# In the stage of the first tiles, ACT makes the first tap of a tile's conv ahead of the silu of the tile before it, from the fifth tile on

## The chip, the cores and the metric

The kernel runs on one core of a Trainium2 chip. The metric is the device time of one execution in microseconds. Five engines work from queues of their own and meet at semaphores: TensorE (PE), VectorE (DVE), ScalarE (ACT), GpSimd (POOL) and SyncE (SP), which issues nearly all DMAs. Each engine takes its instructions in the order in which the kernel lists them.

## The reference

Two transformer blocks run one after the other on 512 tokens of width 1024 (the first adds 16 meta tokens, which makes 528). The change touches only the head of the first block:

```python
h = rmsnorm(h_res, norm1_w)
proj = h @ w_in                       # q, k, v (1024 columns each), z, b, a, ...
qkv = silu(depthwise_conv_centred(concat([q, k, v]), conv_w))   # 5 taps along the tokens
q, k = l2norm(q) * 128 ** -0.5, l2norm(k)       # 8 heads of 128
o = chunk_gated_delta_rule(q, k, v, g, beta)    # forward and backward
```

The delta rule needs, for each chunk and head, products of k with k and with q, the inverse of a triangular matrix made of them, and k and v with the tokens on the partitions.

## The kernel before

Channels lie on the partitions and tokens along the free axis. Matrices are cut in units of 128 output columns by 1024 inputs. To come near float32 with the fast number format, each unit is split in a rounded part `w_hi` (ACT, `round_unit`, line 383) and the rest `w_lo` (POOL, `split_unit`, line 389), and so are the activations; a product is three passes, hi by hi, lo by hi, hi by lo (`gemm`, line 401).

The stage of the first tiles runs over the 24 entries of `TILES`: 0 to 3 are heads 0 to 3 of k, 4 to 7 heads 0 to 3 of q, 8 to 11 and 12 to 15 heads 4 to 7 of k and q, and 16 to 23 the eight heads of v. Every engine has a loop over n = 0 to 24 in its own program, and all loops list their work tile by tile. For tile n:

- PE (`pe_program`, from line 1437) makes 48 matmuls into one of two pairs of PSUM banks, pair n % 2. It first waits until the conv of tile n-2 has read that pair (`cv`, four increments per tile). The last matmul raises `s_pe` to n+1.
- ACT (`act_program`, line 1741, loop from line 1768) rounds the weights of unit n+2, makes the silu of tile n-1 (line 1774, it waits for the four steps of conv n-1 and raises `si`), and then the first of the five taps of tile n (line 1783): a scaled copy from PSUM to the buffer `cacc[:, n % 2]`. The tap waits for `s_pe` at n+1 (for tiles 0 to 3, for DVE's scaling of the tile, `fd`), and for silu n-2, which was the last to read that buffer. It raises `m_tap`. Then come the square of q for a q tile (line 1794) and ACT's part of the side tasks.
- DVE (`dve_program`, line 2100) waits for `m_tap` and adds the other four taps (line 2148), each a pass over the tile, then its side tasks.
- POOL splits unit n+2, SP loads the weights of unit n+4.

The table `SIDE` puts other work behind tile n on every engine: transposes of k at n = 4, 5, 10 and 12 (`pe_kt`, line 639, each for two heads), products and exponentials of the chunks (`pg`, `pk`, lines 498 to 567), the inverse of the blocks on DVE in eight parts at n = 16 to 23 (`sub_part`, lines 604 to 618), and transposes of v at n = 18, 20, 22 and 24 (`pe_vt`, line 700, two heads each). `pe_kt` and `pe_vt` wait for the silus of their heads. At n = 10, 12, 18, 20 and 22 the two heads are tiles n-2 and n-1; at n = 4, 5 and 24 the heads are tiles 0 and 1, 2 and 3, 22 and 23. `pe_pk` at n = 8 waits for silu 7. In PE's queue all this lies between gemm n and gemm n+1. ACT's functions use several tables; a table load (`ACT_TABLE_LOAD`) stands directly ahead of the first instruction that needs another table.

When DVE has copied the inverse (`raw<-inv`, line 618), SP writes it to memory and loads it for the next stage, the chunks of the delta rule, which PE opens with line 875 at 240 us.

Of the kernel before, what the change touches and what calls it, by code (L numbers as in the profile page):

```python
# [10 lines left out]
ACT = mybir.ActivationFunctionType  # L11
# [7 lines left out]
HALF = T1 // 2  # L19
# [61 lines left out]
TILES = [("k", h) for h in range(4)] + [("q", h) for h in range(4)] + [("k", h) for h in range(4, 8)] + [("q", h) for h in range(4, 8)] + [("v", h) for h in range(8)]  # L81
# [44 lines left out]
def build(nc, a, out):  # L126
    ctx = ExitStack()
    with ctx:
        def sem(name):
            return ctx.enter_context(nc.semaphore(name))  # L130
# [25 lines left out]
        def z(name, shape, off, dt=F32):  # L156
            n = int(np.prod(shape[1:])) * 4
            assert z0 + off + n <= nc.sbuf_usable_end, (name, z0 + off + n, nc.sbuf_usable_end)
            return at(name, shape, z0 + off, dt)
# [55 lines left out]
        cacc = z("cacc", [P, 2, T1], W2)  # L215
# [63 lines left out]
        ps = ctx.enter_context(nc.psum_tensor("ps", [P, 8, 512], F32))  # L279
# [4 lines left out]
        def pcol(name, tile, tap=0):  # L284
            o, n, k = PAR[name]
            return par[:, o:o + n * k].rearrange("p (n k) -> p n k", k=k)[:, tile, tap:tap + 1]
# [4 lines left out]
        def pair(v):  # L291
            return v.rearrange("p (b n) -> p b n", b=2)
# [11 lines left out]
        QKV = {"q": ("cq", qT), "k": ("ck", kT), "v": ("cv", vT)}  # L304
# [3 lines left out]
        s_hi, s_lo, s_pe = sem("s_hi"), sem("s_lo"), sem("s_pe")  # L308
# [8 lines left out]
        si = Signal(sem("s_si"), t=3 * H)  # L317
# [10 lines left out]
        fd = Signal(sem("s_fold"), n1=5, gu=2 * FT, lr=2 * LT)  # L328
# [26 lines left out]
        m_tap, m_eg, m_de, m_kme, m_ksq, m_nk = (Mark(sem(f"m_{n}")) for n in ("tap", "eg", "de", "kme", "ksq", "nk"))  # L355
# [21 lines left out]
        def round_unit(e, u):  # L377

            if u < NU:
                e.wait_ge(s_raw[u % RAW], 16 * (u // RAW + 1))  # L380
                if u >= RAW:
                    e.wait_ge(s_pe, u - RAW + 1)
                e.activation(w_hi[:, u % RAW, :], w_raw[:, u % RAW, :], ACT.Copy).then_inc(s_hi, 1)  # L383
# [64 lines left out]
        def query(n):  # L448

            return None if not 0 <= n < len(TILES) or TILES[n][0] != "q" else TILES[n][1]  # L450

        def decays():
            return ps[:, 7, 0:3 * NB * 2 * H].rearrange("p (i c n) -> p i c n", i=3, c=NB)
# [200 lines left out]
        def act_kt(e, hf):  # L654
            e.wait_ge(*m_ktm.at(hf))
            e.wait_ge(*hh.at("n1", KT))
            e.activation(k_met[0:META, HG * hf:HG * hf + HG, :], bankv(4, META, P), ACT.Copy).then_inc(m_kme.sem, 1)

        def act_n2(e, hf):
            e.wait_ge(*m_kte.at(HG * hf + 3))  # L660
            e.wait_ge(*m_kme.at(hf))
            if hf:
                e.wait_ge(*m_nc.at(1))
            e.activation(ksq[:], k_tok[:, hf].rearrange("p c u m -> p (c u) m"), ACT.Square).then_inc(m_ksq.sem, 1)
            e.activation(ksq_m[0:META], k_met[0:META, HG * hf:HG * hf + HG, :], ACT.Square).then_inc(m_ksq.sem, 1)
# [1075 lines left out]
        def act_program(e):  # L1741
            o, n, _ = PAR["norm1"]
# [20 lines left out]
            def first_hi(k):  # L1763
                e.wait_ge(*hh.at("n1", k + 1))
                e.activation(h_hi[:, k, :], hf0[:, k, :], ACT.Copy).then_inc(hi.sem, 1)


            for n in range(len(TILES) + 2):
                if n < len(TILES):
                    round_unit(e, n + 2)  # L1770
                if 1 <= n <= len(TILES):
                    what, h = TILES[n - 1]
                    e.wait_ge(*cv.at("t", 4 * n))
                    e.activation(QKV[what][1][:, h, :], cacc[:, (n - 1) % 2, :], ACT.Silu).then_inc(si.sem, 1)
                if n < len(TILES):
                    what, h = TILES[n]
                    b = 2 * (n % 2)
                    for k in (0, 1, 2) if n == 2 else ():
                        first_hi(k)
                    e.wait_ge(*(fd.at("n1", (1, 2, 4, 5)[n]) if n < 4 else (s_pe, n + 1)))  # L1780
                    if n >= 2:
                        e.wait_ge(*si.at("t", n - 1))
                    e.activation(pair(cacc[:, n % 2, :]), ps[:, b:b + 2, 0:HALF], ACT.Copy, scale=pcol(QKV[what][0], h)).then_inc(m_tap.sem, 1)  # L1783
                    if n == 2:
                        for k in range(3, KT):
                            first_hi(k)
                i = query(n - 1)
                if i is not None:
                    e.wait_ge(*si.at("t", n))
                    if i >= HG:  # L1790
                        e.wait_ge(*m_qs.at(0))
                    if i == HG:
                        e.wait_ge(s_qn, 16)
                    e.activation(qsq[:, i % HG, :], qT[:, i, META:T1], ACT.Square).then_inc(sq.sem, 1)
                for task, arg in SIDE.get(n, ()):
                    if task == "bat":
                        e.wait_ge(*dg.at("b", 1))
                        e.activation(beta[:], beta[:], ACT.Sigmoid).then_inc(ga.sem, 1)
                        e.activation(small[:, 32:48], small[:, 0:16], ACT.Exp).then_inc(ga.sem, 1)
                        e.wait_ge(*dg.at("ch", 3))  # L1800
                        e.activation(tmpc[:, 1, :], tmpc[:, 1, :], ACT.Exp).then_inc(ga.sem, 1)
                    if task == "dk":
                        e.wait_ge(*pg.at("dk", 1))
                        for i in range(3):
                            e.activation(tabs[:, i], decays()[:, i], ACT.Exp if i else ACT.Copy).then_inc(ga.sem, 1)
                    if task == "ktm":
                        act_kt(e, arg)
                    if task == "ks":
                        act_n2(e, arg)
                    if task == "nk":  # L1810
                        act_nk(e)
                    if task == "vt":
                        act_vt(e, arg)
                    if task == "vtm":
                        act_vtm(e, arg)
                    if task == "msa":
                        act_msa(e, arg)
                    if task == "msb":
                        act_msb(e, arg)
                    if task == "pg":  # L1820
                        act_pg(e, arg)
                    if task == "qs":
                        act_qs(e, arg)
                    if task == "mk":
                        act_mg(e)
# [222 lines left out]
            for g in range(LT // 3 + 1):  # L2048
                n, last = 7 * g + BASE["xr0"], g == LT // 3
# [666 lines left out]
```

## Time and profile before

| | us |
|---|---|
| median of 3 runs | 1828.39 |
| lowest and highest | 1827.64, 1830.20 |
| the profiled execution, its own time | 1829.92 |
| its span | 1828.1 |
| PE busy | 1747.4 |
| DVE busy | 824.5 |
| ACT busy | 679.7 |
| POOL busy | 861.4 |
| mean granted clock of PE | 0.975 |

The span is what the profiler recorded, from the first instruction to the last; the time of an execution holds a little more. Every row of a timeline gives the start in us from the start of the span, the length in us, engine, line, operation and the tiles written and read (`out<-in`); x8 says that eight instructions were merged. In brackets stands how long the engine had stood idle and who released it.

### The profile page before, as it was taken

The page shows a single profiled execution, that of the slowest core. Times are in us where ns is not written, and L with a number is a line of the kernel's source. Part 1 is how long each engine was busy: PE and PEld are TensorE (multiplying, and loading weights), DVE is VectorE, ACT ScalarE, POOL GpSimd, SP SyncE. Part 2 cuts the span into 40 slices and gives each one's busy share as a digit, 9 for nine tenths or more (in the row PEclk, how much of TensorE's full clock was granted, in tenths as well). Part 3 has the DMA queues.
Part 4 walks back from the last instruction along what each step waited for, and adds up shares of the span by engine and source line. Part 5 has one row for each costly group of instructions (what it writes and reads, how often), then busy time and mean ns, then how long its engine had stood idle before and what let it go on. Part 6 is the DMA issues. An engine that isn't in the chain of part 4 may idle for free.

```text
span 1828.1 us, 22823 instructions
## 1 busy us (share of the span) xinstructions
PE 1747.4 (96%) x9151; PEld 1473.5 (81%) x9151; DVE 824.5 (45%) x1323; ACT 679.7 (37%) x997; POOL 861.4 (47%) x482
## 2 busy tenths in 40 slices
PE   7899869999999999999999999989999999999987
PEld 7888869998988888877888878868887788877766
DVE  7668925923323301122111121127999842457642
ACT  5656523332332222233222232233233443365651
POOL 3356423232334644544555554445477645456552
PEclk9899969999999999999999999989999989999998
DMA  5475258463422324222222223322222312222222
GB/s 193 136 226 164 70 155 254 133 173 110 145 70 71 96 98 140 92 93 92 93 93 92 93 92 104 104 70 93 94 98 89 112 58 93 92 93 92 93 74 76
DMA packets 120145, 201.41 MB, mean 110 GB/s; under 512 B 32448, under 2 KB 71512, under 8 KB 120040
## 3 DMA queue, kind: packets, MB, share of 16 engines
q1 hardware_dynamic: 118552, 197.47, 34.3%
q10 hardware_dynamic: 1488, 2.48, 0.4%
q8 instruction: 73, 1.20, 0.3%
q14 instruction: 32, 0.26, 0.0%
HBM read 170.46 MB, written 29.46 MB: 109 GB/s over the span
## 4 chain that ended last, share of the span: by engine, by line
PE 85%; DVE 9%; ACT 3%; issue 2%; DMA 1%; POOL 1%; SPq 0%; DVEq 0%; ACTq 0%
PE ps L401 67%; PE ps L1733 3%; DVE cacc L2148 2%; PE ps L875 2%; PE ps L921 1%; PE ps L928 1%; PE ps L907 1%; PE ps L885 1%; PE ps L915 1%; PE ps L883 1%; PE ps L932 1%; PE ps L893 1%; DVE inv L615 1%; DVE ps L1341 1%; PE ps L1680 1%
## 5 line engine op out<-in xcount | busy, mean ns | idle before, releaser
L389 POOL TENSOR_TENSOR w_lo<-w_raw,w_hi 128x1024 fp32r<-128x1024 f32 x264 | 632.8, 2406 | 567.0 <-ACT w_hi L383 566.9
L401 PE MATMUL ps<-hp_hi,w_hi 128*128 128x512 f32 (+2 forms) x1664 | 558.2, 363 | 7.3 <-DVE cacc L2148 6.1
L401 PE MATMUL ps<-hp_lo,w_hi 128*128 128x512 f32 (+2 forms) x1664 | 553.3, 360 | 0.0
L401 PE MATMUL ps<-hp_hi,w_lo 128*128 128x512 f32 (+2 forms) x1664 | 553.2, 360 | 0.0
L401 PEld LDWEIGHTS ps<-hp_hi,w_hi 128*128 128x128 f32 x1664 | 297.7, 191 | 63.2 <-issue 7.5
L401 PEld LDWEIGHTS ps<-hp_lo,w_hi 128*128 128x128 f32 x1664 | 297.1, 190 | 50.3 <-issue 1.7
L401 PEld LDWEIGHTS ps<-hp_hi,w_lo 128*128 128x128 f32 x1664 | 297.4, 190 | 48.0
L383 ACT ACTIVATE w_hi<-w_raw 128x1024 fp32r<-128x1024 f32 x264 | 277.5, 1053 | 152.0 <-DMA w_raw<-in_w 144.3
L1221 DVE SCALAR_TENSOR_TENSOR ps<-u_in,par,ps 128x511 f32<-128x511 f32 (+14 forms) x240 | 176.7, 739 | 8.4 <-ACT ps L1213 0.8
L2148 DVE SCALAR_TENSOR_TENSOR cacc<-ps,par,cacc 128x528 f32<-128x528 f32 x96 | 73.6, 767 | 37.3 <-ACT cacc L1783 34.6
L2524 POOL TENSOR_TENSOR y_lo<-tmp,y_hi 128x512 fp32r<-128x512 f32 x22 | 28.4, 1289 | 105.6 <-ACT y_hi L1932 105.6
L401 PE MATMUL ps<-y_hi,w_hi 128*128 128x512 f32 x176 | 69.6, 396 | 1.5 <-DVE tmp L2284 1.5
L1929 ACT ACTIVATE tmp<-tmp 128x512 f32<-128x512 f32 x22 | 13.9, 632 | 150.8 <-DVE tmp L2277 150.8
L401 PE MATMUL ps<-y_hi,w_lo 128*128 128x512 f32 x176 | 69.5, 395 | 0.0
L401 PE MATMUL ps<-y_lo,w_hi 128*128 128x512 f32 x176 | 69.5, 395 | 0.0
L2279 DVE TENSOR_TENSOR ps<-ps,tmp 128x512 f32<-128x512 f32 x22 | 15.4, 699 | 103.8 <-PE ps L401 103.8
L401 PE MATMUL ps<-mx_hi,w_hi 128*128 128x512 f32 x144 | 57.4, 398 | 0.0
L401 PE MATMUL ps<-mx_lo,w_hi 128*128 128x512 f32 x144 | 57.1, 397 | 0.0
L401 PE MATMUL ps<-mx_hi,w_lo 128*128 128x512 f32 x144 | 57.0, 396 | 0.0
L2277 DVE TENSOR_TENSOR tmp<-tmp,ps 128x512 f32<-128x512 f32 x22 | 15.1, 687 | 92.5 <-PE ps L401 85.7
L943 ACT ACTIVATE TR<-ps 128x512 f32<-128x512 f32 x32 | 19.1, 597 | 89.9 <-PE ps L875 89.9
L2309 DVE TENSOR_TENSOR x<-x,ps 128x512 f32<-128x512 f32 x8 | 5.5, 686 | 102.1 <-PE ps L401 102.1
(397 smaller groups left out, 2575.5 us busy)
## 6 DMA issues: line engine op xcount, KB each, us to landing
w_raw<-in_w SPq DMA_DIRECT2D x264, 512.0 KB, 3.5
d_y<-zero SPq DMA_DIRECT2D x6, 688.0 KB, 6.1
d_x<-zero SPq DMA_DIRECT2D x6, 688.0 KB, 5.9
d_at<-at SPq DMA_DIRECT2D x16, 256.0 KB, 3.0
d_kc<-kc SPq DMA_DIRECT2D x16, 256.0 KB, 3.2
d_qd<-eg SPq DMA_DIRECT2D x16, 256.0 KB, 3.1
d_p<-dec SPq DMA_DIRECT2D x16, 256.0 KB, 3.4
AT<-d_at SPq DMA_DIRECT2D x16, 256.0 KB, 6.1
```

Of the source, the lines that this page charges most:

```text
L383: e.activation(w_hi[:, u % RAW, :], w_raw[:, u % RAW, :], ACT.Copy).then_inc(s_hi, 1)
L389: e.tensor_tensor(w_lo[:, u % RAW, :], w_raw[:, u % RAW, :], w_hi[:, u % RAW, :].bitcast(F32), ALU.subtract).then_inc(s_lo, 1)
L401: mm = e.matmul(ov, w, r[:, k, t0:t1], start=(first and n == 0 and p3 == 0), stop=(last and n == len(tiles) - 1 and p3 == 2))
L615: e.tensor_tensor(inv[:, j + 1:, 0:w], inv[:, j + 1:, 0:w], prd, ALU.subtract).then_inc(m_sub.sem, 1)
L875: mm = e.matmul(bankv(LB[s], P, P)[:, u], SQ[s]["AT"][:, u], SQ[s]["X"][:, u], start=True, stop=True)
L883: e.matmul(half_cols(LB[s], 0)[:, u], T[:, u], blocks(Y, 1 - s)[:, u], start=True, stop=True)
L885: mm = e.matmul(half_cols(LB[s], 1)[:, u], Y[:, u], blocks(T, s)[:, u], start=True, stop=True)
L943: e.activation(SQ[s]["TR"][:], bankv(LB[s], P, P), ACT.Copy).then_inc(q_tc[s].sem, 1)
L1221: e.scalar_tensor_tensor(acc[:, t:SEQ], u_in[:, k, 0:SEQ - t], pcol("ca", k, TAPS - 1 - t), acc[:, t:SEQ], ALU.mult, ALU.add).then_inc(cl. ...
L1733: mm = e.matmul(ps[:, LBANK[j], :], w, r[:, k, :], start=(k == 0 and p3 == 0), stop=(k == LT - 1 and p3 == 2))
L2148: e.scalar_tensor_tensor(acc, ps[:, b:b + 2, t:t + HALF], pcol(QKV[what][0], h, t), acc, ALU.mult, ALU.add).then_inc(cv.sem, 1)
L2524: e.tensor_tensor(y_lo[:, j - 1, :], row(2 + (j - 1) % 2), y_hi[:, j - 1, :].bitcast(F32), ALU.subtract).then_inc(lo.sem, 1)
```

## The change

From the fifth tile on (n = 4), ACT makes tap n before silu n-1; before, the silu came first. The tap's code moves into a function `act_tap`, with the same waits and the same operands. For n below 4 the order stays. The other engines' programs are untouched. Nothing is added or taken away.

```diff
+            def act_tap(n):
+
+                what, h = TILES[n]
+                b = 2 * (n % 2)
+                e.wait_ge(*(fd.at("n1", (1, 2, 4, 5)[n]) if n < 4 else (s_pe, n + 1)))
+                if n >= 2:
+                    e.wait_ge(*si.at("t", n - 1))
+                e.activation(pair(cacc[:, n % 2, :]), ps[:, b:b + 2, 0:HALF], ACT.Copy, scale=pcol(QKV[what][0], h)).then_inc(m_tap.sem, 1)
 
             for n in range(len(TILES) + 2):
                 if n < len(TILES):
                     round_unit(e, n + 2)
+                if 4 <= n < len(TILES):
+                    act_tap(n)
                 if 1 <= n <= len(TILES):
                     what, h = TILES[n - 1]
                     e.wait_ge(*cv.at("t", 4 * n))
                     e.activation(QKV[what][1][:, h, :], cacc[:, (n - 1) % 2, :], ACT.Silu).then_inc(si.sem, 1)
-                if n < len(TILES):
-                    what, h = TILES[n]
-                    b = 2 * (n % 2)
+                if n < 4:
                     for k in (0, 1, 2) if n == 2 else ():
                         first_hi(k)
-                    e.wait_ge(*(fd.at("n1", (1, 2, 4, 5)[n]) if n < 4 else (s_pe, n + 1)))
-                    if n >= 2:
-                        e.wait_ge(*si.at("t", n - 1))
-                    e.activation(pair(cacc[:, n % 2, :]), ps[:, b:b + 2, 0:HALF], ACT.Copy, scale=pcol(QKV[what][0], h)).then_inc(m_tap.sem, 1)
+                    act_tap(n)
```

## Rows read from the trace of the kernel before

**Rows 1.** The page, part 1: busy time, share of the span, instructions.

```profile
PE 1747.4 (96%) x9151; PEld 1473.5 (81%) x9151; DVE 824.5 (45%) x1323; ACT 679.7 (37%) x997; POOL 861.4 (47%) x482
```

**Rows 2.** Busy time in two stretches: PE, PEld, DVE, ACT, POOL, granted clock, DMA.

```profile
168.00:228.00 60.00, 55.67 (x410) 50.60 (x409) 56.19 (x101) 31.90 (x73) 29.41 (x42) 0.97 0.23 72
300.00:1828.00 1528.00, 1489.09 (x7243) 1227.54 (x7241) 617.39 (x918) 527.73 (x742) 729.46 (x372) 0.99 0.31 99
```

**Rows 3.** The chain of waits at the end of the stage: start, length, what.

```profile
213.42 7.70 PE ps L401 x48
221.14 0.71 ACT cacc L1783
...
226.49 1.05 DVE raw L618
...
240.10 2.05 PE ps L875 x8
```

**Rows 4.** The tap's line 1783: its waits, and who waited for it.

```profile
  PE ps L401: 27.7, 12
...
  DVE cacc L2148: 34.6, 13
```

**Rows 5.** Timeline of ACT at tile 14.

```profile
150.32 1.28 ACT L1774 ACT_TABLE_LOAD   x1
...
152.16 0.68 ACT L1783 ACTIVATE cacc<-ps,par 128x528 f32<-128x528 f32 x1
```

**Rows 6.** Timeline of PE behind gemm 8.

```profile
94.20 2.00 PE L507 MATMUL ps<-kT 128*128 128x128 f32 x8 [2.35 <-ACT qT L1774]
```

**Rows 7.** Timeline of ACT at tiles 18, 20 and 22.

```profile
179.88 1.28 ACT L1774 ACT_TABLE_LOAD   x1
181.17 0.64 ACT L1774 ACTIVATE vT<-cacc 128x528 f32<-128x528 f32 x1
182.97 0.70 ACT L1783 ACTIVATE cacc<-ps,par 128x528 f32<-128x528 f32 x1 [1.15 <-PE ps L401]
...
195.51 0.65 ACT L1774 ACTIVATE vT<-cacc 128x528 f32<-128x528 f32 x1 [3.55 <-DVE cacc L2148]
196.06 0.68 ACT L1783 ACTIVATE cacc<-ps,par 128x528 f32<-128x528 f32 x1
...
211.09 0.64 ACT L1774 ACTIVATE vT<-cacc 128x528 f32<-128x528 f32 x1 [5.98 <-DVE cacc L2148]
```

**Rows 8.** Timeline of PE: what lies between the gemms of tiles 18 to 23.

```profile
182.76 1.04 PE L700 MATMUL ps<-cf,vT 128*128 128x128 f32 x8
...
189.62 0.38 PE L706 MATMUL ps<-cf,vT 128*16 128x128 f32 x2
...
195.84 1.04 PE L700 MATMUL ps<-cf,vT 128*128 128x128 f32 x8
...
208.93 0.60 PE L700 MATMUL ps<-cf,vT 128*128 128x128 f32 x4
211.79 0.66 PE L700 MATMUL ps<-cf,vT 128*128 128x128 f32 x4 [2.26 <-ACT vT L1774]
212.38 1.04 PE L818 MATMUL ps<-v_met,m_dec 16*16 16x128 f32 x8
```

**Rows 9.** Timeline of DVE: the convs of tiles 19, 21 and 23.

```profile
192.31 3.17 DVE L2148 SCALAR_TENSOR_TENSOR cacc<-ps,par,cacc 128x528 f32<-128x528 f32 x4
...
207.90 3.17 DVE L2148 SCALAR_TENSOR_TENSOR cacc<-ps,par,cacc 128x528 f32<-128x528 f32 x4
...
221.88 3.18 DVE L2148 SCALAR_TENSOR_TENSOR cacc<-ps,par,cacc 128x528 f32<-128x528 f32 x4 [0.58 <-ACT cacc L1783]
```

**Rows 10.** Busy time in two stretches, columns as in rows 2.

```profile
213.80:217.20 3.40, 3.40 (x17) 3.40 (x16) 3.26 (x6) 2.46 (x8) 0.87 (x1) 0.50 0.00 0
...
94.30:97.70 3.40, 3.40 (x17) 3.40 (x17) 3.26 (x7) 1.90 (x3) 3.32 (x4) 0.50 0.80 304
```

**Rows 11.** Groups of DVE's instructions from 148 to 228 us, costliest first.

```profile
L2148 DVE SCALAR_TENSOR_TENSOR cacc<-ps,par,cacc 128x528 f32<-128x528 f32 x40 | 30.6, 766 | 6.9 <-ACT cacc L1783 5.9
```

## The prediction

> **What bounds the kernel now.** I read the page first: PE is busy 96% of 1828.1 us [rows 1], and from 300 us to the end it stands still for only 39 of 1528 us [rows 2]. What happens before 240 us therefore moves all that follows, one for one. The stage of the first tiles ends at 240.10 us, when PE starts the next stage after standing still since 227 us. The reader sees in the chain of waits what that start hangs on: gemm 23, tap 23, conv 23, the rest of the block solve, the copy `raw<-inv` at 226.49 us, its DMAs, then PE [rows 3]. From 168 to 228 us DVE is busy 56.2 of 60 us and PE 55.7 [rows 2]; the two are nearly level, and either can set the end.
>
> "Gemm n", "tap n", "silu n" and "conv n" mean tile n's 48 matmuls, its first tap on ACT (line 1783), its silu on ACT (line 1774) and its four steps on DVE (line 2148). Over the stage DVE waited 34.6 us for taps, and the taps 27.7 us for PE [rows 4]. So a tap is often late because its gemm is late, and only a tap that stands behind a silu can gain.
>
> **The change part by part.** It adds and removes no instruction. From tile 4 on, 20 taps move ahead of 20 silus, and with each silu its table load, if it has one. The units' rounding stays in front of both, so the weights' loads and POOL's splits keep their place; no DMA moves. Two costs trade places:
>
> - Tap n no longer waits for conv n-1, the load and silu n-1. Gain on DVE.
> - Silu n-1 now waits for gemm n, as tap n does, and whoever wants silu n-1 waits too. Behind it on ACT stand the square of q, the exponentials and the copies. On PE, right behind gemm n, the transposes of k at tiles 10 and 12 and of v at tiles 18, 20 and 22 wait for it: the second of each pair needs silu n-1. The products k·k and q·k behind gemm 8 need silu 7.
>
> *Up to tile 17.* Gain: load and silu 13 stand ahead of tap 14 (150.32 us and 152.16 us [rows 5]), worth 1.8 us. Loss: the transposes behind gemm 10 and 12 wait for their silu, and PE's wait for silu 7, now 2.35 us until 94.20 us [rows 6], grows by a tap of 0.6 us and by about 0.5 us that ACT is already late. By the same steps as below gemm 13 comes some 2.1 us late, half of which hides in waits of PE for DVE's copies, and the exponentials that wait for DVE behind it put ACT 1.8 us back in front of tap 14. Gain and loss cancel: tap 14 stays at 152.2 us. At tile 16 tap 16 (one load and silu earlier) no longer holds DVE, which is then 0.55 us early; this is what the change earns and carries into tile 18. Bounds for this half: -1.8 us (all of the gain) and +2.1 us (none absorbed). I take the cancelled value, since DVE's own work between tiles 14 and 16 is long.
>
> *Tile 18.* Before, load and silu 17 (179.88 and 181.17 us) lie beside gemm 18, and tap 18 waits for PE until 182.97 us [rows 7]. PE runs all eight transposes from 182.76 us and gemm 19 right behind [rows 8]. Now tap 18 stays at 182.97 us, and load and silu 17 follow: 182.97 + 0.60 + 1.28 + 0.65 = 185.5 us (0.60 us is a tap's place in the queue, its 0.70 us less the overlap with the next). Transposes of v1, before at 183.2 us, start at 185.55 us: **PE +2.35 us**. Gemm 19 ends with the row at 189.62 us [rows 8]; it comes to 191.97 us, tap 19 to 192.2 us, conv 19 to 192.9 us. Before it began at 192.31 us [rows 9]; DVE was 0.55 us early, and the loss there is only 0.6 us.
>
> *Tile 20.* Gemm 20 ends at 195.84 us [rows 8] + 2.35 = 198.2 us; tap 20 at 198.4 us, before at 196.06 us right behind silu 19 at 195.51 us [rows 7]. Silu 19 is done at 198.4 + 0.6 + 0.65 = 199.65 us, and the transposes of v3, before at 196.28 us, start there: **PE +3.4 us**. DVE does not feel it: conv 21 follows DVE's own work at 207.90 us [rows 9] + 0.6, while tap 21 is ready at 206.4 us.
>
> *Tile 22.* Gemm 22 ends at 208.93 us [rows 8] + 3.4 = 212.3 us; tap 22 at 212.5, silu 21 done at 212.5 + 0.6 + 0.65 = 213.75 us. Before it ended at 211.09 + 0.65 = 211.74 us [rows 7], and PE waited 2.26 us for it until 211.79 us [rows 8]. That wait swallows 1.4 of the 3.4 us: **PE +2.0 us**. Gemm 23 and tap 23 (221.14 us [rows 3]) and conv 23 (221.88 us [rows 9]) follow at once: 223.9 us. DVE is free at 221.9 us and waits. Nothing behind it has slack: copy, DMAs and PE at 240.10 us come 2.0 us later.
>
> **The sum with the clock as it was: +2.0 us.** The profiled execution took 1829.92 us (span 1828.1 us and 1.8 us around it), 1.5 us above the median of 1828.39 us; such differences between runs are of the size of this result.
>
> *The clock.* Not all of it is fixed. Before gemm 23 PE waited 2.26 us and then made only transposes and matmuls of 16 rows [rows 8]; after that 17 matmuls took 3.4 us at a granted clock of 0.50, the 1.2 GHz level [rows 10]. So gemm 23 took 7.70 us [rows 3] where gemm 19 takes about 6.0 (from the end of the transposes at 183.6 to 189.6 us [rows 8]): one such stretch is worth 1.7 us. PE's wait of 2.35 us from 91.8 us also had one behind it, at 94.3 us [rows 6, 10]. After the change a new wait of 2.35 us with transposes around it stands ahead of gemm 19, as long as the two that had a stretch behind them: I expect one there. On PE's path it adds 1.7 us: gemm 19 ends at 193.7 us, v3's transposes start at 201.4 us, gemm 22 ends at 214.0 us, silu 21 at 215.5 us, everything 1.7 us behind the walk above; DVE, 2.3 us late from conv 19 on, stays just inside. The old stretch may go, since PE's wait ahead of gemm 23 shrinks to 1.1 us; but the light work behind the wait stays. The four cases at the end: none of the two +0.3 us, one of them +2.0 us (either one), both +3.7 us. I take the new one whole and 1.2 of the old one's 1.7 us, **+3.2 us**, nearer to both than to one because only the wait shrinks and not the light work. The Trainium skill's page "TensorE: Matmul & The Clock Gate", Part 1, says the clock falls to half after PE was little busy, and that the monitor runs free of the kernel's start; by it the same wait can have a slow stretch behind it in one run and none in another. The rows agree for two waits; one trace cannot show the second part.
>
> The page "ScalarE: Activation LUTs", section "What ACT_TABLE_LOAD costs", speaks against the change: it puts a switch at 1283 ns and a drain of some 1380 ns more. By it silu 17, moved with its load behind tap 18, would be done 1.38 us later, and the same walk gives +3.4 us where the clock stays as it was. The trace disagrees: silu 17 starts 1.29 us after its load does [rows 7].
>
> **Rivals.**
>
> 1. *More slow stretches.* PE's wait for silu 7 grows to 3.5 us and that for silu 17 is new; each may leave two stretches behind it instead of one. It decides from both stretches of the forecast whole plus any part of a third: 3.7 us, 1832.1 us, at its lower end, 2.0 + 1.7 + 1.7 = 5.4 us, 1833.8 us, with a third, 7.1 us with a fourth. For it: from 168 us on PE has 4.3 us of 60 in which to hide anything [rows 2]. Against: a stretch at 94 us is mostly absorbed by tile 14, as above.
> 2. *The early taps win.* If PE's waits at tiles 18 and 20 stay hidden behind DVE, only the gain stands: 0.55 us at tile 16 and the 0.58 us that DVE waited for tap 23 [rows 9], 1.1 us, 1827.3 us. Against: it needs gemm 23 1.1 us early, and it hangs on silu 21 behind gemm 22. The most that taps can give after 148 us is 6.9 us of DVE's idle time [rows 11], 1821.5 us; that needs PE to be early at every tile.
> 3. *It does nothing.* 12 taps already waited for PE [rows 4], and if the transposes' waits found slack as well, the time stays at 1828.4 us.
> 4. *A load costs more where it follows a tap.* If silu 17 came 1.4 us later than its rows say: 3.4 us on the walk, with the clock's 1.2 us 4.6 us, 1833.0 us.
>
> **How the numbers follow.** A measurement of this kernel can tell about 0.2%, 3.7 us, from no change. Forecast, between +0.3 and +3.7 us: 0.47. Rival 1, from both stretches whole upwards: 0.40. Rivals 2 and 3 within 0.2%: 0.07; rival 2 beyond it: 0.04. Rival 4: 0.02. Predicted: 1828.39 + 3.2 = 1831.6 us. The range starts with the forecast's smallest case, +0.3 us, 1828.7 us, and goes nearly to a fourth stretch, 1835.0 us. Faster 0.04, same 0.47 + 0.07 = 0.54, slower 0.40 + 0.02 = 0.42.
>
> **What the profile would show.** Right: taps 18, 20 and 22 wait for PE with load and silu behind them; PE waits some 2.4 us ahead of the transposes at 183 us and about 1 us at 199 and 213 us; DVE's longest wait late in the stage is the one for tap 23, some 2 us; clock rows of 0.50 stand behind 186 us and perhaps 214 us; `raw<-inv` starts 2 to 4 us later than 226.49 us; behind 240 us everything is shifted and nothing else differs. Wrong: if the transposes at 183 us don't wait, the walk falls at its first step; if they do and the copy is on time, DVE set the end; if the copy is early, rival 2 holds; if it is over 4 us late, the clock's rows say how many stretches.

## The result and the profile after

The changed kernel takes 1832.21 us in the median of 20 runs (1830.37 to 1835.35), the kernel before, run beside it, 1828.07 us (1826.24 to 1831.74, 20 runs). The ratio is 1.0019, with a 95% interval from 1.0013 to 1.0025: 3.5 us more by the ratio (2.4 to 4.6 us), 4.1 us by the medians. Forecast were 1831.6 us and 1828.7 to 1835.0 us.

The profiled execution of the changed kernel took 1830.97 us, its span is 1829.1 us. That is 1.0 us above the span of before, less than the medians differ by. Two things make it so. Of the two slow stretches of PE (stretches at a granted clock of 0.50) that the forecast counted on, this execution had neither. And it was ahead before the new order had cost anything: its conv 6 starts 46.5 us after conv 0, that of before 49.6 us, and a run below with the order of before (e7_before_fill) has 46.6 us as well; before had a slow stretch at 70.4 us that this execution had not. From conv 6 to the copy `raw<-inv` the changed kernel takes 151.2 us and before 148.1 us, 3.2 us more, which is near what the medians say.

The page's first part answers [rows 1]; the windows answer [rows 2, 10] and the second and third rows add the places where the slow stretches had been expected (columns: window, its length, busy time and instructions of PE, PEld, DVE, ACT and POOL, granted clock, DMA share, GB/s):

```profile
PE 1745.7 (95%) x9151; PEld 1470.2 (80%) x9151; DVE 826.8 (45%) x1323; ACT 679.5 (37%) x997; POOL 861.5 (47%) x482
```

```profile
92.00:98.80 6.80, 5.79 (x26) 5.80 (x27) 6.52 (x13) 2.52 (x4) 6.44 (x6) 0.50 0.39 143
184.90:188.30 3.40, 2.95 (x24) 2.96 (x25) 3.23 (x7) 3.40 (x10) 0.10 (x1) 1.00 0.19 70
212.90:217.00 4.10, 3.29 (x26) 2.81 (x27) 3.87 (x8) 4.10 (x15) 0.00 (x0) 1.00 0.39 128
168.00:228.00 60.00, 54.93 (x406) 49.88 (x404) 56.98 (x98) 29.64 (x65) 28.85 (x41) 0.98 0.23 72
300.00:1828.00 1528.00, 1490.10 (x7252) 1227.67 (x7251) 617.88 (x919) 527.75 (x742) 730.32 (x373) 0.99 0.31 99
```

Between 168 and 228 us DVE is busy 0.8 us more than before, PE 0.8 us less. At 185 us and at 213 us the granted clock is 1.00; the stretch at 213.8 us of before [rows 10] is gone. At 92 us PE is at 0.50 for 6.8 us, where before had 3.4 us from 94.3 us on.

On ACT the timeline of the changed kernel at tile 18 answers [rows 7] (start, length, engine, line, operation, tiles; in brackets the idle time before it and who ended it). Line 1774 is now the tap, line 1785 the silu:

```profile
182.64 0.70 ACT L1774 ACTIVATE cacc<-ps,par 128x528 f32<-128x528 f32 x1 [3.10 <-PE ps L401]
183.36 1.28 ACT L1785 ACT_TABLE_LOAD   x1
184.65 0.64 ACT L1785 ACTIVATE vT<-cacc 128x528 f32<-128x528 f32 x1
```

On PE, for silu 7 and for the transposes behind gemm 18, 20 and 22, the same view answers [rows 6, 8]:

```profile
93.00 2.08 PE L507 MATMUL ps<-kT 128*128 128x128 f32 x8 [3.68 <-ACT qT L1785]
182.44 0.60 PE L700 MATMUL ps<-cf,vT 128*128 128x128 f32 x4
185.35 0.66 PE L700 MATMUL ps<-cf,vT 128*128 128x128 f32 x4 [2.31 <-ACT vT L1785]
199.54 0.66 PE L700 MATMUL ps<-cf,vT 128*128 128x128 f32 x4 [0.89 <-ACT vT L1785]
213.71 0.66 PE L700 MATMUL ps<-cf,vT 128*128 128x128 f32 x4 [0.89 <-ACT vT L1785]
```

Each second head's transposes now wait for a silu that stands behind a tap: 2.31, 0.89 and 0.89 us, where the forecast had 2.4, about 1 and about 1. But PE does not set the end in this execution. The chain of waits (start, length, what) runs through DVE, whose shares among the lines between 180 and 245 us are 27.8% for the convs and 42.6% for the block solve; [rows 3] had PE's gemm 23 in its place. Of its pieces:

```profile
188.69 2.48 DVE inv L615
196.00 1.46 DVE prd L612
204.04 1.22 DVE prd L612
217.77 2.49 DVE prd L612
227.15 1.06 DVE raw L618
```

Most steps of the solve at these widths take 0.4 us; these four took 1.2 to 2.5 us. Conv 23 starts at 222.55 us without a wait, the copy `raw<-inv` at 227.15 us, 0.66 us behind [rows 3]. The prediction had named this sign: if the transposes wait and the copy is on time, DVE set the end. From the copy on the two traces are nearly alike (1602.0 us to the end, before 1601.6 us); from 300 us PE is busy for 1490.10 us, 1.0 us more than [rows 2].

### The profile page after: what moved, and what is told of

The parts are those of the page before. It is cut to its first block, busy times and chain, and to the rows that moved or that the text cites. A ratio compares the mean times of both kernels' runs of the same rounds, so it can differ in the third digit from the quotient of the medians.

```text
span 1829.1 us, 22823 instructions
## 1 busy us (share of the span) xinstructions
PE 1745.7 (95%) x9151; PEld 1470.2 (80%) x9151; DVE 826.8 (45%) x1323; ACT 679.5 (37%) x997; POOL 861.5 (47%) x482
## 3 DMA queue, kind: packets, MB, share of 16 engines
q10 hardware_dynamic: 1488, 2.48, 0.4%
## 4 chain that ended last, share of the span: by engine, by line
PE 80%; DVE 8%; issue 2%; ACT 1%; POOL 1%; SPq 0%; DMA 0%; DVEq 0%; ACTq 0%
PE ps L401 64%; PE ps L1733 3%; DVE cacc L2154 2%; PE ps L875 2%; PE ps L921 1%; DVE inv L615 1%; PE ps L928 1%; PE ps L915 1%; PE ps L907 1%; PE ps L885 1%; PE ps L883 1%; DVE prd L612 1%; PE ps L932 1%; PE ps L893 1%; DVE ps L1341 1%
```

## The experiments

A kernel's time is given with its range and number of runs, and the ratio to the kernel before, run on the same chip, with its 95% interval. In the traces I also measured two distances, since a run's start differs by some tenths of a us: the first half is from the start of conv 0 to that of conv 18 (the orders up to tile 17 and their after-effects), the second half from conv 18 to `raw<-inv`. Where another line number stands below, it is the same instruction moved by the inserted lines.

### Which half costs

In the kernel before the silu stands ahead of the tap; here a set, `AHEAD`, says for which tiles the tap stands ahead: 18 to 23 in e1_late, 4 to 17 in e2_early, 14 and 16 in e3_two. The cut shows the edit of the changed kernel.

```diff
-                if 4 <= n < len(TILES):
+                if n in AHEAD:
                     act_tap(n)
...
-                if n < 4:
+                if n < len(TILES) and n not in AHEAD:
```

> The tap stands ahead of the silu only for tiles 18 to 23. My theory (PE's transposes of v wait for the silu that now stands behind the tap, and the clock falls behind the new wait): nearly the whole loss, +2.0 us by the walk at the clock as it was, +2.5 to +4 us with slow stretches; `raw<-inv` at about 228.5 us where gemm 23 has its slow stretch. Rival (the loss is made in the first half, at the wait for silu 7 and at the transposes of k, and its slow stretches): within 0.7 us of the kernel before.

e1_late measured 1833.0 us (1830.9 to 1833.8, 11 runs), ratio 1.0020 (1.0010 to 1.0029), some 3.7 us more, within what was expected of slow stretches. Its profiled execution is the case "both stretches" of the forecast. The chain of waits, then two windows:

```profile
184.56 7.49 PE ps L402 x48
192.28 6.01 PE ps L402 x48
...
215.42 7.69 PE ps L402 x48
223.14 0.71 ACT cacc L1775
...
228.49 1.06 DVE raw L619
```

```profile
185.40:188.80 3.40, 3.40 (x18) 3.40 (x17) 3.30 (x5) 1.46 (x4) 1.86 (x1) 0.50 0.01 2
216.10:219.50 3.40, 3.40 (x18) 3.40 (x17) 3.29 (x5) 1.58 (x4) 1.74 (x1) 0.50 0.00 0
```

Gemm 19 and gemm 23 take 7.49 and 7.69 us beside 6.01 us for gemm 20; tap 23 comes last and DVE waits 1.34 us for it. The second half takes 45.58 us as against 41.83 us before: +3.7 us, the forecast's sum for "both". So the walk on PE through tiles 18, 20 and 22 is borne out, in one execution, for the case in which both stretches fall and PE sets the end.

The same run shows something that had not been looked for. Up to tile 17 its code is that of before, and yet its conv 18 starts 152.9 us after conv 0, where before has 155.8 us. The windows of the two kernels at 70 us, before first:

```profile
70.40:73.80 3.40, 3.40 (x18) 3.40 (x17) 1.39 (x3) 3.37 (x5) 0.85 (x1) 0.50 0.49 181
```

```profile
70.00:77.00 7.00, 7.00 (x59) 6.92 (x58) 1.87 (x4) 5.59 (x9) 2.41 (x1) 1.00 0.32 105
```

One execution had a slow stretch there, the other had none: 18 matmuls in 3.4 us against 59 in 7.0 us. Of the 2.9 us, 1.5 us arise between conv 5 and conv 6, which are 11.0 us apart in before and 9.5 us in e1_late, where this stretch lies. The other 1.4 us are there at conv 5 already; the two executions have slow stretches ahead of it as well, which fall at 22.6 and 56.8 us in before and at 21.5 and 55.7 us in e1_late, but no run isolates their part. The Trainium skill, "TensorE: Matmul & The Clock Gate", Part 1, says that the monitor runs free of the kernel and that the number of slow matmuls varies from run to run; these two rows agree.

> The tap stands ahead of the silu only for tiles 4 to 17. My theory: the half is neutral, gain at tile 16 against losses that are absorbed at tile 14: -0.5 us, up to +1 us if the longer wait for silu 7 leaves a second slow stretch. Rival (the loss is made in this half): +2 to +4 us.

e2_early measured 1832.38 us (1828.77 to 1835.16, 11 runs), ratio 1.0018 (1.0010 to 1.0027). This is a miss, and what the rival had: the first half of the change costs by itself nearly what the whole does. Its trace has PE's wait for silu 7 and, behind it, a slow stretch of 6.8 us (PE's timeline, then the window):

```profile
97.02 2.08 PE L508 MATMUL ps<-kT 128*128 128x128 f32 x8 [3.68 <-ACT qT L1786]
```

```profile
95.80:102.60 6.80, 5.58 (x25) 5.59 (x26) 6.59 (x12) 2.73 (x4) 6.44 (x6) 0.50 0.44 156
```

Conv 18 comes 158.5 us after conv 0, 2.7 us later than before. The two halves cost about 1.0018 and 1.0020 by themselves and 1.0019 together. So they don't add up: a late start of the second half, or its slow stretches, may hide behind one another. That is a reading: the intervals are about 1.7 us to each side, and leave room for this to be scatter.

> The tap stands ahead of the silu at tiles 14 and 16 alone, the two at which no transposes and no products on PE want the silu at once and at which a table load stood ahead of the tap. My theory: the gain without the loss. Tap 14 at about 150.6 us where it was at 152.2, `raw<-inv` about 2.0 us earlier, -1 to -2 us in all. Rival (taps are not what DVE waits for in the long run, since gemm and DVE's own work are level): 0 us within 0.5.

e3_two (only taps 14 and 16, the ones that stood behind a load or a silu without waiting for PE) measured 1828.99 us (1826.91 to 1833.07, 11 runs), ratio 1.0001 (0.9992 to 1.0011): a miss too, no gain shows in the median. In the trace conv 18 is 1.4 us earlier than before (154.4 us after conv 0), and the second half is 1.8 us longer: 0.9 us of it are DVE's waits behind a slow stretch of 6.8 us in place of 3.4 us (window, then DVE's timeline), the other 0.9 us are longer steps of the block solve (see "Where the solve loses it"):

```profile
211.80:218.40 6.60, 6.46 (x28) 5.29 (x29) 6.29 (x12) 5.44 (x16) 1.36 (x1) 0.50 0.04 14
```

```profile
223.45 3.18 DVE L2155 SCALAR_TENSOR_TENSOR cacc<-ps,par,cacc 128x528 f32<-128x528 f32 x4 [1.44 <-ACT cacc L1775]
```

### Does the wait for silu 7 make the first half's loss

```diff
+AHEAD = set(range(4, 24)) - {8}          # e5_not8
+AHEAD = set(range(4, 18)) - {8, 10, 12}  # e6_early_free
```

> The changed order on tiles 4 to 23 except tile 8, where the silu stays ahead of the tap, so that the products behind gemm 8 get silu 7 as before. The half with tiles 4 to 17 lost 3.7 us where I had expected none; its profile and that of the changed kernel show PE waiting 3.7 us for silu 7 and 6.8 us of half clock behind, where the kernel before has 2.35 and 3.4 us. My theory now: this wait and its second slow stretch are what the first half loses, and the second half loses its own 2 to 3.7 us: the whole falls from +4.1 to +2.5 us (within 1.5 to 3.5). Rival (the transposes of k at tiles 10 and 12 make the first half's loss): +4 us as before.

> The changed order on tiles 4 to 17 except tiles 8, 10 and 12, where PE wants the silu right behind the gemm. My theory: the loss of the first half sits in these three; without them it is gone: -1.3 to +0.5 us. Rival (something else of the first half costs, such as the later squares of q or exponentials): +2 us or more.

e5_not8 measured 1833.32 us (1832.89 to 1834.66, 7 runs), ratio 1.0027 (1.0016 to 1.0039): a miss. e6_early_free measured 1831.83 us (1825.55 to 1833.36, 11 runs), ratio 1.0009 (0.9998 to 1.0021), which decides nothing. The premise of both failed, as PE's timeline of e5_not8 shows:

```profile
95.01 2.08 PE L508 MATMUL ps<-kT 128*128 128x128 f32 x8 [3.09 <-ACT qT L1786]
```

With tap 8 behind silu 7 again, PE still waits 3.09 us (3.09 us in e6_early_free as well), not 2.35 us [rows 6]: 0.6 us of the 1.3 us more came from the tap of tile 8, the rest from the earlier tiles, after which ACT is late. Both have a slow stretch of 6.8 us at 94 us. Removing one tap takes only half of the growth away.

### PE kept busy in its waits

To take the clock out of the comparison, PE gets matmuls to do where it stands and waits; their results are overwritten. Their number is chosen to fit into the wait. In both functions the wait for the silu now stands behind them, and the waits for free PSUM banks ahead of them.

```diff
@@ helper
+        def keep_busy(e, bank, count, width=HALF + 4):
+            for _ in range(count):
+                e.matmul(ps[:, bank, 0:width], hp_hi[:, 0, 2:2 + P], hp_hi[:, 0, 0:width], start=True, stop=True)
...
@@ pe_pk, behind gemm 8, ahead of the wait for silu 7 (16 in e7_before_fill)
+            keep_busy(e, 6, 20 if x == 0 else 0)
@@ pe_vt, ahead of the second head's transposes at tiles 18, 20, 22 ((0, 0, 14) in e7_before_fill)
+                if i == 1 and p < 3:
+                    keep_busy(e, 5, (16, 6, 6)[p])
```

> The changed kernel, with matmuls of no use (268 columns, the result is overwritten by the transposes or products behind them) laid in PE's waits: 20 ahead of the products that need silu 7, and 16, 6 and 6 ahead of the second head's transposes of v at tiles 18, 20 and 22. They end before the waits do. My theory: the waits stay, the slow stretches behind them go: the clock's share of the loss, 1 to 2.5 us, comes back, so +1.5 to +3 us against the kernel before instead of +4. Rival (the whole loss is the waits themselves): as the changed kernel, +4 us. A second rival (the matmuls delay the transposes): +5 us or more.

e4_fill, the changed kernel with this, measured 1829.34 us (1828.52 to 1833.13, 11 runs), ratio 1.0003 (0.9994 to 1.0012): 2.9 us less than the changed kernel. The direction is confirmed, the size is not quite: some 0.5 us above before where 1.5 to 3 us were expected, with an interval that reaches to 2.2 us. Its trace, of its slowest execution (1833.13 us), has no slow stretch behind any of the waits that the change lengthens, at 92, 185 and 213 us.

> The kernel before, with matmuls of no use in PE's two waits that had a slow stretch behind them: 16 ahead of the products that need silu 7, 14 ahead of the transposes of v5 at tile 22. The order on ACT is that of before. My theory (a stretch costs 1.7 us where PE is on the path): both go, -1.5 to -3 us, `raw<-inv` at most 195.5 us behind the first conv where the kernel before has 197.6. Rival (the filled kernel gained for another reason, such as the silu's wait moved in PE's queue): 0 us.

e7_before_fill, the same for the kernel before, measured 1827.85 us (1825.46 to 1828.91, 11 runs), ratio 0.9997 (0.9988 to 1.0006), a miss: by the ratio before gains only 0.5 us. The profiled execution, its fastest at 1825.46 us, had only one slow stretch in the stage and `raw<-inv` 192.6 us after conv 0, 5 us before that of the kernel before. So the filler takes 2.9 us off the changed kernel and 0.5 us off before: by these ratios the clock has a part of about 2.4 us in the change's loss. With intervals of 1.6 us to each side for the two and 1.1 us for the change, this is not clear of nothing.

The traces say it more closely. Before, e8_gap (the run below, with the same filler behind gemm 8), e2_early and e4_fill are level at conv 6, 49.6 to 49.8 us after conv 0. From there to conv 18 before takes 106.2 us, with 3.4 us at 0.50 behind its wait for silu 7, and e8_gap 104.7 us, with none. With taps 4 to 17 moved e2_early takes 108.7 us, with 6.8 us at 0.50, and e4_fill 105.8 us, with none. The windows of e8_gap and then e4_fill in this place:

```profile
91.00:99.00 8.00, 7.63 (x63) 7.41 (x62) 7.79 (x10) 5.48 (x8) 6.27 (x5) 1.00 0.50 156
92.00:99.00 7.00, 5.80 (x48) 5.57 (x48) 6.90 (x9) 6.53 (x9) 4.23 (x3) 1.00 0.57 176
```

So the half clock behind silu 7 costs 1.5 us in the old order and 2.9 us in the new one, all of it still there at conv 18, and the new order alone costs 1.1 us up to there. The other traces agree within 0.2 us: 106.2 us in e1_late and 108.5 us in the changed kernel with the half clock, 104.9 us in e7_before_fill without it.

> As the run before, and 48 matmuls of 512 columns of no use in PE's 13 us of waiting at the end of the stage, 36 from about 227 us and 12 behind the scatter. In the kernel before the clock is at 0.50 from 230.8 to 254.7 us, of which PE works 14.6 us. My theory: these run at full clock, 6 to 7 us less, and perhaps the stretch at 261.6 us with it: -8 to -11 us against the kernel before. Rival (the slots are bound by DMAs and by DVE and ACT between PE's steps, so that the clock there costs nothing): as the run before.

```diff
@@ on e7_before_fill: PE's idle time at the end of the stage, ahead of the chunks
+            if lev == 32 and s == 0 and k == 0:
+                e.wait_ge(*cv.at("t", 4 * 24))
+                for count, done in ((36, 64), (12, 0)):
+                    keep_busy(e, LB[0], count, SEQ)
+                    if done:
+                        e.wait_ge(s_sca[0], done)
```

e8_gap measured 1820.95 us (1820.59 to 1822.13, 5 runs), ratio 0.9961 (0.9948 to 0.9973): 7 us below before (4.9 to 9.5 us), and 6.9 us below e7_before_fill in the medians. That is some 1 us short of the 8 to 11 us expected; the 6 to 7 us for the half clock alone fit. PE's timeline and the window behind 232 us, and the window of the kernel before in the same place:

```profile
225.15 8.56 PE L504 MATMUL ps<-hp_hi 128*128 128x512 f32 x36
235.55 3.04 PE L504 MATMUL ps<-hp_hi 128*128 128x512 f32 x12 [1.84 <-DMA d_x<-raw]
238.53 1.13 PE L889 MATMUL ps<-X,AT 128*128 128x128 f32 x8
```

```profile
232.00:255.00 23.00, 17.19 (x122) 14.90 (x121) 5.03 (x14) 8.49 (x19) 6.05 (x5) 1.00 0.69 199
```

```profile
240.00:254.70 14.70, 14.60 (x64) 13.24 (x65) 0.57 (x2) 7.30 (x17) 2.28 (x2) 0.50 0.53 164
```

Before, PE starts the chunks at half clock after 13 us of idleness and makes 64 matmuls in 14.7 us; with the filler the clock is 1.00 throughout and the first eight take 1.13 us as against 2.05 us [rows 3].

### The orders with the clock held up

The last four kernels put filler into all these places (and 28 matmuls ahead of gemm 5), each around another order: f1_before that of before, f2_after that of the change, f3_early with taps 4 to 17 ahead, f4_two with taps 14 and 16. The counts fit each one's waits: 16 matmuls ahead of silu 7 (22 in f2_after and f3_early), and at tiles 18, 20 and 22 the numbers of e4_fill in f2_after, of e7_before_fill in the others.

```diff
@@ all four: the filler of e8_gap at the end of the stage, and this ahead of gemm 5
+                    if n == 5:
+                        e.wait_ge(*dg.at("ch", 1))
+                        keep_busy(e, 6, 28)
```

> A measuring kernel: the order of the kernel before, with matmuls of no use in all of PE's long waits up to the next stage (28 of 268 columns ahead of gemm 5, 16 ahead of the products that need silu 7, 14 ahead of v5's transposes, 36 and 12 of 512 columns at the stage's end), so that only one or two slow stretches are left to chance. Expected 7 to 9 us below the kernel before, and little scatter from run to run. The three kernels beside it carry the same filling with another order on ACT; the differences to this one are the orders' own cost, without the clock.

> The changed kernel with its waits filled (22 ahead of the products, 16, 6 and 6 ahead of the transposes at tiles 18, 20 and 22, the rest as in the measuring kernel). My theory (the walk: silus behind late gemms hold PE's transposes): +2.0 us against the measuring kernel with the order of before, within 1.2 to 2.8; what the changed kernel loses beyond that, some 2 us, is the clock. Rival (the loss of 4.1 us is all waits): +3.5 to +4.5 us. Rival (it is all clock): +0.5 us or less.

> The changed order on tiles 4 to 17 alone, waits filled (22 ahead of the products, else as the measuring kernel). My theory (at the clock held up, the first half loses 1 to 2 us at tiles 8 to 13 and gains it back at 14 to 16): -0.5 us against the measuring kernel, within -1.3 to +0.5; then the +3.7 us of the same order without filling were slow stretches. Rival (the delays of the first half are not absorbed): +1.5 to +3 us.

> The tap ahead of the silu at tiles 14 and 16 alone, waits filled as in the measuring kernel. My theory (here a tap is freed from a load and a silu and nobody on PE wants the silu at once): -2.0 us against the measuring kernel, within -1.2 to -2.5, and the fastest of all. Rival (a gain of taps is lost behind PE in the second half): 0 within 0.5 us.

| | median us (range, runs) | ratio to before (95%) | first half | second half | copy after conv 0 |
|---|---|---|---|---|---|
| f1_before | 1823.71 (1822.84 to 1823.97, 6) | 0.9972 (0.9961 to 0.9983) | 154.3 | 41.02 | 195.3 |
| f2_after | 1826.44 (1822.32 to 1828.52, 12) | 0.9983 (0.9974 to 0.9991) | 154.3 | 42.74 | 197.0 |
| f3_early | 1825.33 (1824.07 to 1826.77, 11) | 0.9981 (0.9972 to 0.9989) | 155.3 | 41.19 | 196.5 |
| f4_two | 1822.27 (1820.93 to 1824.11, 5) | 0.9965 (0.9953 to 0.9977) | 151.3 | 41.56 | 192.9 |

f1_before gains 5 us over before where 7 to 9 us were expected, less than e8_gap without the filler ahead of gemm 5; that is a miss. Against f1_before the whole change still costs 2.7 us in the medians (2.0 us in the ratios), as expected. Its first half costs 1.6 us, a miss (-0.5 us were expected), and every run of f3_early is longer than every run of f1_before. Taps 14 and 16 alone are 1.4 us faster, as expected, but the runs of the two kernels overlap.

The clock is not level even here. Seven of f2_after's twelve runs have a mean granted clock of 0.981 or 0.982 and take 1826.3 to 1828.5 us, the other five, at 0.984 or 0.985, 1822.3 to 1825.0 us; f1_before has 0.983 or 0.984 in all six. So a part of the 2.7 us is still the clock. Likewise two of f4_two's five runs, at 0.983, take 1823.9 and 1824.1 us, no less than f1_before, and the other three, at 0.985, 1820.9 to 1822.3 us. The traces differ too: at 70 us a stretch at 0.50 is 6.8 us long in f1_before and f3_early and 3.4 us in f2_after and f4_two. So f3_early is to be compared with f1_before (first half +1.0 us), and f2_after's equal first half hides about as much, since its conv 6 was 1.1 us earlier: from conv 6 to conv 18 it takes 105.8 us, as f3_early and e4_fill do, and f1_before 104.8 us. In the second half the only slow stretch is one in f2_after from 224.0 us, behind the start of its conv 23 (222.49 us), and there f2_after stands 1.7 us behind f1_before. No wait of DVE explains that: it stands still for 2.04 us between conv 18 and the copy in both. The groups of DVE's instructions between 168 and 232 us do (line, tiles, count, busy us, mean ns, idle before), f1_before first, then f2_after:

```profile
L621 DVE TENSOR_TENSOR inv<-inv,prd 128x31 f32<-128x31 f32 (+15 forms) x31 | 15.2, 491 | 1.1
L618 DVE TENSOR_TENSOR prd<-blk,inv 128x31 f32<-128x31 f32 (+15 forms) x31 | 13.1, 423 | 0.8
```

```profile
L621 DVE TENSOR_TENSOR inv<-inv,prd 128x31 f32<-128x31 f32 (+15 forms) x31 | 15.2, 492 | 1.1
L618 DVE TENSOR_TENSOR prd<-blk,inv 128x31 f32<-128x31 f32 (+15 forms) x31 | 14.8, 479 | 0.8
```

The same 62 instructions take 28.3 us in the one and 30.0 us in the other: 1.7 us, the whole difference. Before and after show it as well: 28.5 and 30.1 us. From conv 18 to the copy the change takes 42.7 to 42.8 us in the four traces that have its order at tiles 18 to 23 and no slow stretch ahead of conv 23 (after, e4_fill, e5_not8, f2_after). Four traces with the order of before in this half and no slow stretch have 41.0 to 41.2 us (e7_before_fill, e8_gap, f1_before, f3_early).

### Where the solve loses it

No run was made for this; the rows show it. POOL and then DVE in the timeline of the changed kernel:

```profile
188.38 2.53 POOL L389 TENSOR_TENSOR w_lo<-w_raw,w_hi 128x1024 fp32r<-128x1024 f32 x1 [3.38 <-ACT w_hi L383]
194.78 2.39 POOL L389 TENSOR_TENSOR w_lo<-w_raw,w_hi 128x1024 fp32r<-128x1024 f32 x1 [0.67 <-ACT w_hi L383]
217.66 2.40 POOL L389 TENSOR_TENSOR w_lo<-w_raw,w_hi 128x1024 fp32r<-128x1024 f32 x1 [6.31 <-ACT w_hi L383]
```

```profile
188.69 2.47 DVE L615 TENSOR_TENSOR inv<-inv,prd 128x220 f32<-128x220 f32 x1
192.83 3.17 DVE L2154 SCALAR_TENSOR_TENSOR cacc<-ps,par,cacc 128x528 f32<-128x528 f32 x4
195.92 1.53 DVE L612 TENSOR_TENSOR prd<-blk,inv 128x247 f32<-128x247 f32 x1
217.69 2.56 DVE L612 TENSOR_TENSOR prd<-blk,inv 128x175 f32<-128x175 f32 x1
```

A step of the solve that starts while POOL splits a unit does not end until the split does: 188.69 + 2.47 = 191.16 us beside 188.38 + 2.53 = 190.91 us; 195.92 + 1.53 = 197.45 us beside 197.17 us. Conv 19, which reads one of its operands from PSUM, runs beside the split from 194.78 us at its usual 3.17 us. In the trace of before the splits of these two tiles fall in this way, POOL and then DVE:

```profile
186.75 2.41 POOL L389 TENSOR_TENSOR w_lo<-w_raw,w_hi 128x1024 fp32r<-128x1024 f32 x1 [1.46 <-ACT w_hi L383]
192.50 2.39 POOL L389 TENSOR_TENSOR w_lo<-w_raw,w_hi 128x1024 fp32r<-128x1024 f32 x1
```

```profile
187.75 1.64 DVE L612 TENSOR_TENSOR prd<-blk,inv 128x207 f32<-128x207 f32 x1
```

The first split overlaps conv 18 (184.66 to 187.83 us) for 1.1 us and costs one step 1.3 us; the second runs from 192.50 to 194.89 us, wholly beside conv 19 (from 192.31 us [rows 9]), and costs nothing. Before is not free of such steps: it has three in the second half (1.64 us, 2.48 us at 205.49 us and 1.67 us at 217.25 us), some 4.7 us more than they need, and the change has four, some 6.3 us more. The first three of the change's four stalled steps stand in each of the five traces with the new order at tiles 18 to 23, to 0.2 us, and in none of the nine others. What moved the splits is ACT's queue (its timeline in the changed kernel):

```profile
185.20 2.15 ACT L722 ACTIVATE v_tok<-ps,nk 128x128 f32<-128x128 f32 x8
187.19 1.11 ACT L383 ACTIVATE w_hi<-w_raw 128x1024 fp32r<-128x1024 f32 x1
```

The copies of v from PSUM stand behind the transposes that PE now makes late, and the rounding on which the split waits stands behind the copies. So the splits come 1.6 and 2.3 us later and fall into the solve. The Trainium skill, "SBUF — State Buffer", section "SBUF: two separate sides", puts it so: DVE and GpSimd share one pair of ports, and an operation of DVE with two inputs in SBUF and one of GpSimd that reads SBUF hold it for a whole instruction each, while the other waits. The rows agree for the solve's steps, which have two such inputs; the conv steps with an operand in PSUM kept their length.

The first half has the same. The changed kernel, DVE:

```profile
161.55 0.81 DVE L674 TENSOR_SCALAR n<-n 128x20 f32<-128x20 f32 x1
170.35 2.52 DVE L604 COPY blk<-raw 64x1024 f32<-64x1024 f32 x1
```

Before, the first took 0.17 us and the second 1.81 us (1.11 us in f4_two, where it starts at 167.83 us, ahead of the split, and the next two steps of the solve take 1.1 us more instead). On POOL an operation runs from 161.30 us for 1.03 us and a split from 169.49 us for 2.40 us. These two have one input each, so the sentence above does not cover them; that they stall under POOL's work rests on the rows alone. The pair is 0.64 + 0.71 = 1.35 us longer than before; f3_early has the same two at 0.84 and 2.48 us, f1_before at 0.17 and 2.00 us, 1.15 us apart.

## Why the prediction was right, and where it was not

**The time, the sign and the range** held: +3.2 us was forecast, +3.5 us (ratio) to +4.1 us (medians) were measured. The parts under this sum held less well.

**Tiles 18, 20 and 22, on PE: right.** Tap 18 with load and silu behind it (forecast 182.97 and 185.5 us at the silu's end; 182.64 and 185.29 us measured), waits of 2.31, 0.89 and 0.89 us, tap 20 at 198.25 us (198.4), tap 22 at 212.43 us (212.5). Conv 19 was expected at 192.9 us and came at 192.83 us.

**The clock: right in kind.** The stretch before gemm 19 and that before gemm 23 exist (e1_late, 7.49 and 7.69 us for gemms of 6.0 us), with both the second half comes +3.7 us late as worked out, and whether one falls is a matter of the single run: the profiled execution of the change had neither. Filling the waits gives back 2.9 us of the change's loss (e4_fill) and 0.5 us of before's time, by ratios with wide intervals. Rival 1, more slow stretches, is true in one place: behind the longer wait for silu 7 (3.68 us; 3.5 us were forecast) the clock stays low for 6.8 us in place of 3.4 us (after, e2_early, e5_not8, e6_early_free). I had put it aside with "a stretch at 94 us is mostly absorbed by tile 14", and that was wrong: the half clock there costs 1.5 us up to conv 18 in the old order (before to e8_gap) and 2.9 us in the new one (e2_early to e4_fill). The sum had nothing for it.

**"DVE does not feel it": the step that failed.** The walk carried the lateness of taps to DVE and nothing else, and so gave +0.3 us for an execution without slow stretches. DVE's own work is not constant: the solve's steps stall for POOL's splits, and the change moves the splits. The sentence behind it that fell is "POOL's splits keep their place": they keep it in the queue, not in time, since the rounding stands behind ACT's copies of late transposes. Where no slow stretch holds it, the second half costs +1.7 us (f2_after to f1_before) and DVE, not PE, sets the end. Between the profiles of before and after the 0.58 us that DVE waited for tap 23 [rows 9] goes and 1.6 us of stalls come: +1.0 us, and 42.78 less 41.83 us is 0.95 us. With slow stretches both there (e1_late) PE sets the end and the stalls hide.

**"Gain and loss cancel" up to tile 17: mis-sized.** Forecast was DVE 0.55 us early. f3_early stands 1.0 us later at conv 18 than f1_before, and its median is 1.6 us longer. At conv 14 it is 0.4 us late: it loses 1.3 us between conv 6 and conv 9 and gets 0.9 us back up to conv 14. Behind that the term left out is again POOL: 1.15 us of stalls between these two, against a gain of 0.6 us at tile 16, near the forecast's 0.55 us.

**The sum again.** In the traces the change takes 3.2 us more from conv 6 to the copy. The order's own part is 1.1 us up to conv 18 and 1.7 us behind it. The clock's part is 2.7 us of half clock behind silu 7 where before has 1.5 us, 1.2 us more, less some 0.8 us that before's own slow stretch at 213.8 us costs it (41.83 us against 41.02 us in f1_before) and this execution did not have: 1.1 + 1.7 + 1.2 - 0.8 = 3.2 us. This is one execution of each; the medians put the order's part at 2.0 to 2.7 us, some clock included, and the clock's at 2.4 us within wide intervals. I had put 2.0 us to PE's waits behind tile 18 and 1.2 us to the clock there. That the total came out near was luck: where no slow stretch falls, an unforeseen cost on DVE took the place of one on PE that DVE hid, and the clock's cost fell at silu 7, where the sum had nothing.

**Rivals 2, 3 and 4.** Rival 2 fell for the whole change. For a selection the traces bear it out: f4_two's first half is 3.0 us shorter than f1_before's, of which 1.4 us are there at conv 6 already, before its order differs, and 1.6 us come behind it; e3_two gains 1.5 us on before between conv 6 and conv 18. The second half of f4_two is 0.5 us longer. That would leave some 1.1 us; the medians have 1.4 us, which is not clear of the scatter of five and six runs, and e3_two shows none. Rival 3 fell with the ratio. Rival 4 fell: behind tap 18 silu 17 starts 184.65 - 183.36 = 1.29 us after its load, the same as with the load beside waiting [rows 7].

**What stays open.** POOL's split was never moved by itself, so its price rests on rows of the traces, not on an experiment. Why the halves alone cost as much as both together (e1_late, e2_early) is settled only as far as the intervals of 1.7 us to each side allow. How e5_not8 comes to +5 us is not explained. Its trace does not help: its `raw<-inv` comes 2.2 us later after conv 0 than that of the changed kernel, but it was 2.7 us later at conv 6 already, and it has a slow stretch at 70.2 us that the changed kernel's execution has not; from conv 6 on it is 0.5 us shorter. So tile 8's order seems to help, and all seven runs lie above 1832.8 us all the same.

## What to carry to other kernels

When an in-order engine gets two instructions swapped, follow both directions: who waits for the one that moved back, and then also which instructions elsewhere now run side by side; an instruction's length in the trace of before holds only as long as its neighbours do. A change of some 0.2% in a kernel with PE waits of 2 to 4 us can't be read from one pair of profiles, since identical code was 2.9 us apart in two executions here; fill the waits with idle matmuls in both kernels, compare those at like granted clock, and count distances in the traces from the last point at which both are level. And where PE stands still for long ahead of a dense stage, the filler is worth more than the order: e8_gap and f4_two, 0.9961 and 0.9965 of the time of before, beat both kernels.

## What the runs showed of the hardware that had not been expected

- 13 us of idleness at the end of a stage cost 7 us behind it, by the clock (e8_gap against e7_before_fill): granted clock 0.50 from 230.8 to 254.7 us in before, 1.00 with 48 matmuls in the gap.
- Behind waits of 3.1 to 3.7 us the half clock lasted 6.8 us in every trace that has them without filler; behind waits of 2.3 us it lasted 0, 3.4 or 6.8 us in different executions.
- A `TENSOR_SCALAR` over 20 columns took 0.81 us in place of 0.17 us, and a step over 175 columns 2.56 us where the next one over 175 took 0.34 us, when POOL was at work; four conv steps with an operand in PSUM kept their 3.17 us beside it.
